# Gate rows of a dense layer and the end of the last expert: an edit of order and engines in a two-layer decoder trunk

## What is computed

```
for l in range(2):
    mod = silu(c) @ ada_w[l] + ada_b[l]
    sh1, sc1, g1, sh2, sc2, g2 = split(mod, 6)
    h = rms_norm(x, norm_mix[l]) * (1 + sc1) + sh1
    x = x + g1 * token_mixing(h, ...)
    h = rms_norm(x, norm_ffn[l]) * (1 + sc2) + sh2
    f = swiglu(h, w1, w3, w2) if l == 0 else sum_e gate[:, e] * swiglu(h, w1[e], w3[e], w2[e])
    x = x + g2 * f
return rms_norm(x, final_norm)
```

## Time and profile before

| what | value |
|---|---|
| median of three runs | 1961.74 us (1961.16 to 1961.96) |
| the profiled execution's own time | 1960.09 us |
| its span | 1958.3 us |
| TensorE matmul busy | 1880.5 us (96%) |
| VectorE busy | 1478.7 us (76%) |
| ScalarE busy | 1143.9 us (58%) |
| mean granted TensorE clock | 0.986 |
| HBM traffic | 272 GB/s over the span |

### The profile page before, as it was taken

One profiled execution on the slowest core, in us unless ns is written; L12 is line 12 of the kernel. 1 busy time (PEld: TensorE's weight loads), 2 busy tenths in 40 slices (PEclk: granted clock), 3 DMA queues, 4 the chain that ended last, 5 costly groups with the idle time before them and its releaser, 6 DMA issues.

```text
span 1958.3 us, 29535 instructions
## 1 busy us (share of the span) xinstructions
PE 1880.5 (96%) x10802; PEld 1438.2 (73%) x10802; DVE 1478.7 (76%) x1531; ACT 1143.9 (58%) x1245; POOL 95.6 (5%) x134
## 2 busy tenths in 40 slices
PE   5999999999999999999999999999999999999996
PEld 3877778789987777787676676766767767667774
DVE  3766576745567665757888889888888898988888
ACT  2554554334435555542667767677677676767773
POOL 0620100000005201000000000000000000000000
PEclk9999999999999999999999999999999999999998
DMA  8846435585557544353999999999999999999993
GB/s 312 304 166 221 170 128 175 204 314 194 189 179 241 211 152 151 125 176 133 340 347 360 350 348 353 350 350 355 341 357 356 337 351 347 360 358 335 358 361 133
DMA packets 275637, 533.09 MB, mean 272 GB/s; under 512 B 10768, under 2 KB 23392, under 8 KB 275424
## 3 DMA queue, kind: packets, MB, share of 16 engines
q1 hardware_dynamic: 275552, 531.91, 76.5%
HBM read 530.83 MB, written 1.05 MB: 272 GB/s over the span
## 4 chain that ended last, share of the span: by engine, by line
PE 83%; DVE 9%; ACT 3%; DMA 2%; DVEq 2%; issue 1%; SPq 1%; ACTq 0%
PE pA L748 17%; PE pA L749 16%; PE pA L750 16%; PE pA L753 8%; PE pO L748 5%; PE pO L749 5%; PE pO L750 5%; PE pO L753 5%; PE pT L806 3%; DVE w_lo L1877 2%; DVE wide_lo L1922 1%; DMA tab<-in_tables 1%; DVEq L2526 1%; ACT w_hi L1455 1%; ACT wide_hi L1455 1%
## 5 line engine op out<-in xcount | busy, mean ns | idle before, releaser
L1922 DVE TENSOR_TENSOR wide_lo<-raw,wide_hi 128x2048 fp32r<-128x2048 f32 x336 | 761.7, 2291 | 120.6 <-ACT wide_hi L1455 101.2
L1455 ACT ACTIVATE wide_hi<-raw 128x2048 fp32r<-128x2048 f32 x336 | 644.5, 1921 | 211.6 <-PE pO L750 118.0
L1455 ACT ACTIVATE w_hi<-raw 128x1024 fp32r<-128x1024 f32 (+1 forms) x242 | 251.5, 1046 | 327.7 <-PE pA L750 223.6
L1877 DVE TENSOR_TENSOR w_lo<-raw,w_hi 128x1024 fp32r<-128x1024 f32 (+1 forms) x242 | 295.5, 1236 | 158.5 <-ACT w_hi L1455 151.0
L748 PE MATMUL pA<-wide_hi,x_lo 128*96 128x512 f32 x896 | 356.3, 398 | 1.7 <-DVE wide_lo L1922 1.0
L749 PE MATMUL pA<-wide_lo,x_hi 128*96 128x512 f32 x896 | 353.7, 395 | 0.0
L750 PE MATMUL pA<-wide_hi,x_hi 128*96 128x512 f32 x896 | 351.1, 392 | 0.0
L748 PE MATMUL pA<-w_hi,h_lo 128*128 128x512 f32 (+2 forms) x560 | 226.7, 405 | 14.9 <-DVE w_lo L1877 10.9
L749 PE MATMUL pA<-w_lo,h_hi 128*128 128x512 f32 (+2 forms) x560 | 217.2, 388 | 0.0
L750 PE MATMUL pA<-w_hi,h_hi 128*128 128x512 f32 (+2 forms) x560 | 217.1, 388 | 0.0
L748 PEld LDWEIGHTS pA<-wide_hi,x_lo 128*96 128x96 f32 x896 | 144.6, 161 | 65.3 <-issue 3.5
(11 more groups left out here) (275 smaller groups left out, 2237.8 us busy)
## 6 DMA issues: line engine op xcount, KB each, us to landing
raw<-in_moe_w SPq DMA_DIRECT2D x336, 1024.0 KB, 6.7
raw<-in_w_in SPq DMA_DIRECT2D x56, 1024.0 KB, 6.3
raw<-in_ada_w SPq DMA_DIRECT2D x48, 1024.0 KB, 6.4
raw<-in_ffn_w SPq DMA_DIRECT2D x33, 1024.0 KB, 5.0
raw<-in_w_out SPq DMA_DIRECT2D x8, 1024.0 KB, 5.0
raw<-in_cmp_k_w SPq DMA_DIRECT2D x4, 1024.0 KB, 7.8
raw<-in_cmp_v_w SPq DMA_DIRECT2D x4, 1024.0 KB, 11.1
raw<-in_w_read_nsa SPq DMA_DIRECT2D x4, 1024.0 KB, 6.0
```

Of the source, the lines that this page charges most:

```text
L1455: return nc.scalar.activation(dst, src, ACT.Copy)
L1877: V.tensor_tensor(w_lo[m][:, 0:n], raw[s][:, i * n:(i + 1) * n], w_hi[m][:, 0:n].bitcast(F32), ALU.subtract).then_inc(raw_done, 1)
L1922: V.tensor_tensor(wide_lo[m][:, :], raw[g][:, :], wide_hi[m][:, :].bitcast(F32), ALU.subtract).then_inc(raw_done, 2)
```

## The change

Dense layer: `gate_row(l, 5, True)` is issued right behind the last `ada_pair`, ahead of the turn of that pair's sum; the waits on the pT banks around it go, and one wait on both pT banks is put into the first down product ahead of its second half, whose outputs are these banks. VectorE copies the gate rows, adds the last columns and scales them ahead of the block's `hidden` and `lo_a`.

Last expert: the product of `yacc` with `gw` and its addition to x are split by token tile (`sums_in`) and put behind the second and the third block. TensorE issues six products of zeros into pA[0] behind the last down product. `scatter` waits for each half of `oe_lo` by itself. The sums of squares go to ScalarE (Square with an accumulator), behind a Sqrt on two columns whose result nobody reads; the folded quarters alternate between two buffers, so that the addition to x has no wait behind it. VectorE waits for the four sums and reduces them at the end of the pass.

```diff
@@ TensorE, dense layer, down
                         for half in range(2):
+                            if f == 0 and half:
+                                evacuated(b.T, T_free, 2)
@@ TensorE, dense layer, loop over BLOCKS
                         if f == 1:
+                            gate_row(l, 5, True)
                             ada_ended(b.hl.n // 2)
                             evacuated(b.O, O_free, 2)
-                            evacuated(b.T, T_free, 2)
-                            gate_row(l, 5, True)
-                            evacuated(b.T, T_free, 2)
@@ TensorE, scatter
-                        evacuated(b.O, O_free, 2)
...
+                                if t == 0:
+                                    o = b.O.n - 2 + half
+                                    pe.wait_ge(O_free[b.O.slot(o)], b.O.before(o) + 1)
@@ TensorE, end of the pass
                         down(True)
+                        for _ in range(6):
+                            mm(pA[0][:, :].rearrange("p (k n) -> p k n", k=CK), zeros[:, :],
+                               zeros[:, :].unsqueeze(1).broadcast_to([P, CK, P]))
                         scatter()
@@ ScalarE, end of the pass
                         outs()
                         skip(b.T, 2)
+                        nc.scalar.activation(nrm[:, 8:10], nrm[:, 0:2], ACT.Sqrt)
...
+                        for t in range(TT):
+                            for half in range(2):
+                                act.wait_ge(x_folded, folds.done(folds.take()))
+                                nc.scalar.activation(spare[2 * t + half], x[:, t, half * W:(half + 1) * W], ACT.Square,
+                                                     accum_out=sq[:, t, half:half + 1]).then_inc(sq_ready, 1)
@@ VectorE, dense layer
+                        if f == 1:
+                            gate_rows_late()
+                            ada_ended(b.hl.n // 2)
+                            ada_scale(l + 1, 8, R_NMIX)
                         hidden(f, n)
                         lo_a(f, n)
-                        if f == 1:
-                            ada_ended(b.hl.n // 2)
-                            gate_rows_late()
-                            ada_scale(l + 1, 8, R_NMIX)
@@ VectorE, last_scattered
-                            ins = V.scalar_tensor_tensor(tmp[:, :], pt[:, :], gate16[:, t, bass.ds(e, 1)], gw[:, cols_], ALU.mult, ALU.mult)
+                            part = (tmp[:, :], a_sb[:, 1, :])[half]
+                            ins = V.scalar_tensor_tensor(part, pt[:, :], gate16[:, t, bass.ds(e, 1)], gw[:, cols_], ALU.mult, ALU.mult)
...
-                            plink(V.tensor_tensor(x[:, t, cols_], x[:, t, cols_], tmp[:, :], ALU.add))
-                            ins = V.tensor_tensor_reduce(x_f.rearrange("p k n -> p (k n)")[:, 0:W], x[:, t, cols_], x[:, t, cols_], 1.0, 0.0,
-                                                        ALU.mult, ALU.add, sq[:, t, half:half + 1])
+                            folds.take()
+                            V.tensor_tensor(x[:, t, cols_], x[:, t, cols_], part, ALU.add).then_inc(x_folded, 1)
                             if half + t == 2:
-                                ins.then_inc(gather_free, 1)
+                                dve.drain().then_inc(gather_free, 1)
@@ VectorE, last expert
+                    def sums_in(t):
+
+                        plink(dve.drain())
+                        plink(V.tensor_tensor(yacc[:, t, :], yacc[:, t, :], gw[:, :], ALU.mult))
+                        plink(V.tensor_tensor(x[:, t, :], x[:, t, :], yacc[:, t, :], ALU.add))
...
                         block()
                         use_wide(2)
+                        if e is None:
+                            sums_in(0)
                         block()
                         use_wide(1)
                         if e is not None:
                             gathered()
                         use_wide(1)
+                        if e is None:
+                            sums_in(1)
...
                         v = use_wide(2)
-                        plink(dve.drain())
-                        for t in range(TT):
-                            plink(V.tensor_tensor(yacc[:, t, :], yacc[:, t, :], gw[:, :], ALU.mult))
-                            plink(V.tensor_tensor(x[:, t, :], x[:, t, :], yacc[:, t, :], ALU.add))
...
                             last_scattered(p * NE + NE - 1, t)
+                        dve.wait_ge(sq_ready, folds.done(folds.n - 1))
+                        V.tensor_reduce(nrm[:, 6:8], sq[:, :, 0:2], AX_X, ALU.add)
```

More of the change, by code:

```diff
@@ L564, in build @@
         yacc_ready = sem("yacc_ready")
+        x_folded = sem("x_folded")
+        sq_ready = sem("sq_ready")
         fin_ready = sem("fin_ready")
@@ L1782, in _ @@
                     passes = act.value_load(flag[0:1, 0:1], min_val=1, max_val=PASSES)
-                    G, gv = Turn(start=FFB + 1), Turn()
+                    G, gv, folds = Turn(start=FFB + 1), Turn(), Turn()
                     def hi_x():
@@ L1830, in _ @@
                     with rounds(act, 0, passes, {b.raw: 42 * NE, b.hl: 84 * NE, b.hl_in: 84 * NE, b.wide_in: 42 * NE, b.T: 18 * NE + 2, b.O: 2 * NE, G: EFB * NE,
-                                                 gv: NE}) as p:
+                                                 gv: NE, folds: 4}) as p:
                         hi_x()
@@ L1852, in _ @@
                         skip(b.T, 2)
+                        nc.scalar.activation(nrm[:, 8:10], nrm[:, 0:2], ACT.Sqrt)
+                        spare = [x_f.rearrange("p k n -> p (k n)")[:, 0:W], rope_t.rearrange("p h d -> p (h d)"),
+                                 *(v.rearrange("p t h d -> p (t h d)")[:, 0:W] for v in (q_aug, k_aug))]
+                        for t in range(TT):
[3 more added lines that the diff above has]
+                                                     accum_out=sq[:, t, half:half + 1]).then_inc(sq_ready, 1)
             root()
@@ L1999, in normalise @@
                     total = nrm[:, 6:8]
+                if parts is not None and not final:
                     link(V.tensor_reduce(total, sq[:, :, 0:parts], AX_X, ALU.add))
@@ L2526, in scattered @@
                             dve.drain().then_inc(gather_free, 1)
-                    pl = Turn()
+                    pl, folds = Turn(), Turn()
                     def plink(ins):
@@ L2587, in _ @@
                     with rounds(dve, 0, passes, {b.raw: 42 * NE, b.hl: 84 * NE, b.hl_in: 84 * NE, b.wide_in: 42 * NE, b.T: 18 * NE + 2, b.O: 2 * NE, av: EFB * NE,
-                                                 aq: 2 * EFB * NE, xv: NE, gv: 2 * NE, ov: 2 * NE, kv: NE, pl: 11}) as p:
+                                                 aq: 2 * EFB * NE, xv: NE, gv: 2 * NE, ov: 2 * NE, kv: NE, pl: 8, folds: 4}) as p:
                         gathered()
```

## The result

The changed kernel takes 1952.07 us in the median (1949.37 to 1953.17), the kernel before 1961.96 on the same chip: a ratio of 0.9942, interval 0.9928 to 0.9957, or 9.9 us less. The forecast was 1955.4, with a range from 1952.6.

A forecast was written before the change was run, and what follows sets the result against it. TensorE, busy end to end in the expert stage, was taken to bound the kernel. Dense layer -4.7, folded sums +2.4 and tail -4.0 gave -6.3 us, set against the median 1961.74: 1955.4 us, range 1952.6 to 1959.0.

The forecast's parts named there:

- So the change can act in three places only: Whole kernel: only TensorE's waits in the dense layer, new VectorE work in the last expert, and the tail count.
- moving TensorE forward moves the stage with it: Dense layer: weights lie ready, so no later weight wait takes back the 4.7 us gain.
- Dense layer: Gate rows between the last modulation pair and its turn: TensorE's waits and slow matmuls go, gain 4.7 us.
- Folded sums: Last expert: two groups moved between blocks each make TensorE start 1.2 us late, +2.4 us for both.
- The first rival: Last expert: VectorE's slack swallows the folded sums at no cost; -8.7 in all, 1953.0 us, chance 0.12.
- Tail: Behind the last expert's last product: a shorter chain to the end, gain 4.0 us, bounds 2.8 and 4.6.
- The wait by halves: Tail, step 2: TensorE waits for the first half of oe_lo instead of both, 0.60 us gained.
- a quarter: Tail, step 4: fold, add and square of one quarter take 1.4 us in place of 2.12.
- the first pair at full clock: Tail, step 3: six products of zeros keep the clock up for the first scatter pair, 0.50 us gained.
- The branch behind the reduction: Tail, step 5: the If and loop's end on VectorE become exposed, costing 0.4 us, bounds 0 and 0.9.
- table load: Tail, in the half-gain rival (chance 0.15): Square needs another table than Sqrt, a 1.28 us load, +0.6 net.
- Slower by code lying otherwise: Expert loop: changed code length and pass ends cost time; at twice 0.9 us a pass, 1968 us; chance 0.07.

The follow-up runs named there:

- the clock held in both kernels: Products of zeros in six pauses of TensorE in layer 1, added to the kernel before (1957.61 us) and to the changed kernel (1951.31 us).
- the kernel with zeros: The kernel before with products of zeros in six pauses of TensorE in layer 1; 1957.61 us, ratio 0.998.
- the two kernels without them: Changed kernel with the fold back in the tail, 1950.76 us; changed kernel with its four operations behind four blocks, 1949.32 us.
- the one execution without the zeros: The changed kernel without the six products of zeros in the tail; 1951.87 us in one execution.
- the dense part alone: Only the dense layer's edits, against the kernel before; 1954.82 us, ratio 0.9967.
- the last expert's part alone: The changed kernel with the dense edit undone; 1960.67 us, ratio 0.9985 against the kernel before.
- eight zeros: The changed kernel with eight products of zeros ahead of the dense layer's first down product; 1957.10 us.
- twelve: The changed kernel with twelve products of zeros ahead of the dense layer's first down product; 1956.42 us.
- sixteen: The changed kernel with sixteen products of zeros ahead of the dense layer's first down product; 1954.88 us.

## Why the prediction missed

**The step that failed** is "So the change can act in three places only". The sum has no term for layer 1's mixers, between the first place and the second: they were put at nothing, since the diff does not touch them. They gave 4.4 us in the profile, all of it clock, and with the clock held in both kernels the difference fell from 9.9 and 9.6 us to 6.3. For the dense stage itself, "moving TensorE forward moves the stage with it" held: its 4.8 us are still there at layer 1's first turn of `y`. Behind that the same pauses stood ahead of clock 1.00 where they had stood ahead of 0.50. The prediction read the clock only where the diff acts. A view of the granted clock over the whole span of the kernel before would have shown three stretches behind pauses, at 582, 664 and 790, and one more at 740 (0.51 from 740.5 to 743.0), that the kernel with zeros puts at 6.1 us together: that is the bound which the range lacked. Half of it below the forecast, some 3 us, would have reached 1952.4, and all of it 1949.3. How much of it an edit gets could not be had from one profile, for executions with the same shift differ.

**What is left of the sum** came out near: -4.8 + 2.4 - 4.5 and the 0.9 us below make -6.0, where -6.3 was put, and 6.3 was measured with the clock held. That is luck in part, since the tail gave 0.5 more than was put and the hand-overs of the experts, put at nothing, took 0.9.

**Dense layer**, -4.7: -4.8 in the stretch. Right, and for the reason given; the gate rows took 2.05, and the wait moved into the first down product cost nothing.

**Folded sums**, +2.4: the two pauses sum to 2.4 for weight loads, and the two kernels without them took 2.4 less from the ten zeros to the last product (1010.59 each, against 1012.99). Right. The first rival ("swallowed") is refuted for two operations in a row and true for one at a time.

**Tail**, -4.0: -4.5. Two terms were too small. The wait by halves: from the start of `oe_lo` to the scatter pass 0.75 us in place of 1.63, so 0.88 where 0.60 was put. And from the first fold to the reduction pass 6.43 us in place of 8.79, so 2.36 where 2.12 was put; a quarter takes 1.39 (1.40 was put), and the sums are there 6.4 us behind the first fold, where 6.5 was put. The other 0.2 is the idle time of 0.21 ahead of the old reduction, which went as well and which the prediction left out. The other two held: `oe_lo` 1.20 earlier (1.18), the first pair at full clock (1.00 from 1933.79 to 1935.00) 0.48 (0.50). The branch behind the reduction is exposed with 0.40 of idle, as taken from its row, which has 0.44 for an If and what stands around it. The cause given for the 0.50 does not hold in the one execution without the zeros: the tail is as long. The earlier `oe_lo` and the wait by halves shorten TensorE's pause from 3.5 us to 1.4, and in the execution seen that was enough for the clock: 1.00 for the first six of the eight scatter products.

**Rivals of the tail and of the code.** Square took no table load of its own here: there is one load of 1.28 us, as before (at 1933.51), and the four Squares, from 1936.18 on, run behind the dummy Sqrt of 1934.81 without another. "Slower by code lying otherwise" is there on a small scale. Of the +3.5 from the ten zeros to the last product, 2.4 are the pauses; some 0.9 come bit by bit where an expert hands over to the next, 0.37 at the first and 0.07 to 0.12 at each of six others. At the first, VectorE stands longer ahead of a split, for nothing that the profile shows; before and then after:

```profile
1095.87 4.50 DVE L1922 TENSOR_TENSOR wide_lo<-raw,wide_hi 128x2048 fp32r<-128x2048 f32 x2 [0.79 <-issue]
```

```profile
1086.65 4.50 DVE L1937 TENSOR_TENSOR wide_lo<-raw,wide_hi 128x2048 fp32r<-128x2048 f32 x2 [1.14 <-issue]
```

Its instructions there are the same. The gap comes with the dense edit, which lies 660 us ahead of it: it is 1.14 in all eleven profiles of kernels that have this edit, among them the dense part alone, and 0.79 in the three of kernels that have not (before, before with zeros, the last expert's part alone). In the dense part alone the hand-overs cost 0.9 us, in the last expert's part alone 0.1. So the dense part is worth some 4 us, the clock of layer 1 apart. That the code's place does it, as the rival has it, is not shown; the code behind the edit lies otherwise, and no run changes that alone.

**What stays open.** Why half clock comes behind one pause and not behind another of the same length, why the executions of the changed kernel lie close together where those of the dense part alone spread over 11 us, and why executions of one kernel fall into groups, no run here shows. That the shift decides it is a guess that the medians fit; the shift alone does not decide it. Shown is that the surplus is layer 1's clock and that work in the pauses removes it: 4.4 us between the two profiles without the zeros, 0.02 with them.

## What to carry to other kernels

Ahead of a forecast, list every stretch in which the granted clock is low, and take what they cost together as an uncertainty on both sides of any edit that shifts the work ahead of them by microseconds. To compare two versions, fill such pauses with products of zeros in both: then the difference is that of the edits. Work for a second engine is put in pieces smaller than its reserve between two deliveries: four times 1.2 us were free where twice 2.75 cost 2.4.

## What was not expected of the hardware

A pause of 2.98 us does not settle the clock behind it: of the profiles here with the same pause for the same `y`, the eight turns behind it took 1.55 us in the kernel before, 1.09 in the changed kernel both times, 1.20 with eight zeros, 1.97 with twelve and 1.09 with sixteen. Nor does the shift: the dense part alone, as far ahead as the changed kernel, took 1.97. And what comes ahead of layer 1 differs as well: the stretch from the start to the dense layer's last pair, which no edit here touches, took from 416.17 to 422.42 us in the fourteen profiles.
